# Decays of a state-space mixer: one prefix sum as rows, fetched by transfers, for TensorE products per group

## The chip, the cores and the metric

The kernel runs on one core of a Trainium2 chip. The metric is the device time of one execution in microseconds (us). Before the change three runs gave 3154.31, 3154.56 and 3155.26 us, with a median of 3154.56 us.

## The reference, cut to what matters

The program is one inference step of a hybrid decoder layer on 256 prompt tokens (two chunks of 128) and 8 samples of 8 tokens (64 rows), together 320 token columns. The part around the change is the chunked scan of the Mamba-2 mixer, with 64 heads in 8 groups of 8:

```python
Acum = jnp.cumsum(dt * A.reshape(G, R), axis=2)
seg = Acum[:, :, :, None] - Acum[:, :, None]
Lmat = jnp.exp(jnp.where(causal, seg, -jnp.inf))
CB = jnp.einsum('bclgn,bcsgn->bclsg', Cm, Bm)
Wm = CB[..., None] * Lmat * dt[:, :, None]
y_diag = jnp.einsum('bclsgr,bcsgrp->bclgrp', Wm, x)
decay_end = jnp.exp(Acum[:, :, -1:] - Acum)
...
y_off = jnp.einsum('bclgn,bcgrpn,bclgr->bclgrp', Cm, h_prev, jnp.exp(Acum))
```

Two tables of decays are needed for every group. The first is `exp(Acum[l] - Acum[s])` for all pairs of tokens of a chunk: for each head a matrix with s on the partitions and l along the row. Its raw material is the row `Acum[l]`, repeated on every partition, less a per-partition value `Acum[s]`. The second is `exp(Acum[l])`, one row per head, repeated on the 64 partitions of the head. Projections around the scan are plain matrix products; the rest of the layer (short convolution, mixing, ConvFFN, gated embedding, norms) is not touched.

## The kernel before, in words

Every large product runs as three matmuls (lines 1351 to 1353): weights and activations are each split into a high part (`whi`, `n_hi`, `c_hi`) and a low part (`wlo`, `n_lo`, `c_lo`). Weights arrive in pieces of 128x1024 values (512 KB) in a ring of four slots. SyncE issues the loads (line 540), ScalarE makes the high part three pieces ahead of their use (line 595), VectorE the low part (line 874).

The program is a list of segments, each a list of steps, and each engine walks the same list in order; semaphores join them. The order is written out by hand in `ssm_steps`. One pass of the segment "ssm" handles one group: six units x0 to x5 (a unit is one tile of 128 output columns of the input projection, two weight pieces, 48 matmuls), in the middle of them the norm and the eight output products of the group before, then

unit z0, step `ssd1`, unit z1, steps `ssd2` and `ssd3`, `pair` 0, unit z2, `pair` 1, unit z3, `pair` 2, `pair` 3.

Group 0 is written out; groups 1 to 7 are a loop. Per engine, the steps around the change do this:

- TensorE in `ssd1` transposes x (line 1604) and B (1608), forms C times B (1612), and runs `quad` 0. A `quad` (line 1499) is the row `Acum[l]` of four heads on all partitions, made by multiplying a broadcast column of `hcol` with the triangular mask `tri`. In `ssd2` it runs `quad` 1 to 4 and the sums for `ea` (lines 1633 and 1634). In `ssd3` it forms the chunk states (1641 to 1645). In `pair` it transposes two old states (1655), then waits for `w_ready` and forms y_diag (1667), the new sample states (1676) and y_off (1683, 1688).
- VectorE in `ssd1` scales x into `xdt`, `xwf` and `xwe` (line 923, seven operations), masks C times B (`cbm`, 1033 and 1035), subtracts the column for quad 0 (`quad_min`, line 947) and spreads B (`bblk`, 1038). In `ssd2` it does `quad_min` for quads 1 to 4 and multiplies the exponentials with `cbm` into the weights `wm` (1050). Its part of a unit x is a four-tap convolution (914, 917, 919).
- ScalarE in `ssd2` takes the exponential of `wm` (757) and of `ea` (762).
- GpSimd in `pair` multiplies old states with the last columns of `ea` (1283).

## Time and profile before

| quantity | value |
|---|---|
| median of three runs | 3154.56 us |
| span of the profiled execution | 3152.0 us |
| TensorE matmul busy | 3051.6 us (97%) |
| VectorE busy | 1747.5 us (55%) |
| ScalarE busy | 1155.4 us (37%) |
| GpSimd busy | 235.8 us (7%) |
| mean granted TensorE clock | 0.987 |
| bytes moved | 445.44 MB, mean 141 GB/s |
| HBM written | 25.33 MB |

The span is from the first to the last instruction of the one profiled execution. The page gives no other time for that execution; the median of the unprofiled runs lies 2.56 us above its span. A fp32 matmul shows as two records of TensorE. Records of neighbours overlap, since matmuls are pipelined, so what one costs is read from the distance between starts, not from its length. The chain that ended last lies 93% on TensorE.

### The profile page before, as it was taken

To read this page: it belongs to the slowest core of one execution; us is meant where nothing else is said; L and a number is where in the kernel's file an instruction comes from. 1 tells how busy PE (TensorE), PEld (TensorE's weight loads), DVE (VectorE), ACT (ScalarE), POOL (GpSimd) and SP (SyncE) were. 2 spreads that over 40 slices of the span, in tenths; PEclk is the share of its full clock that TensorE was granted. 3 is DMA by queue.
4 is the path that set the end of the run, shared out by engine and by line. 5 is a ranking of instruction groups with operands and counts; after the bars stand their busy time and mean duration, and the time that the engine had idled before them with its cause. 6 is when DMAs were issued, how large, how long until landed. Compare 5 with 4: busy or idle time off the path is not lost.

```text
span 3152.0 us, 54097 instructions
## 1 busy us (share of the span) xinstructions
PE 3051.6 (97%) x20531; PEld 2948.7 (94%) x20531; DVE 1747.5 (55%) x2346; ACT 1155.4 (37%) x1643; POOL 235.8 (7%) x418
## 2 busy tenths in 40 slices
PE   4999999999999999999999999999999999999988
PEld 2989999898989899999999999999999999999988
DVE  3756556565657565455555555565555555555564
ACT  2443433333434333333333333443333333333443
POOL 1020111101010101000000000100000000000110
PEclk9999999999999999999999999999999999999989
DMA  4544545453544445555555555445555455555443
GB/s 120 134 125 124 159 113 161 111 153 109 158 122 136 124 124 181 150 149 155 147 146 147 147 156 142 143 130 153 152 148 146 146 151 150 152 146 147 146 137 113
DMA packets 749596, 445.44 MB, mean 141 GB/s; under 512 B 18154, under 2 KB 746450, under 8 KB 748754
## 3 DMA queue, kind: packets, MB, share of 16 engines
q1 hardware_dynamic: 668488, 396.17, 44.3%
q10 hardware_dynamic: 80969, 47.21, 5.2%
q8 instruction: 113, 1.85, 0.2%
q14 instruction: 26, 0.21, 0.0%
HBM read 417.99 MB, written 25.33 MB: 141 GB/s over the span
## 4 chain that ended last, share of the span: by engine, by line
PE 93%; DVE 3%; issue 1%; SPq 1%; DMA 1%; ACT 1%; ACTq 0%; POOL 0%; POOLq 0%; DVEq 0%
PE ps L1351 27%; PE ps L1353 27%; PE ps L1352 27%; PE ps L1676 2%; PE ps L1688 2%; PE ps L1667 2%; PE ps L1506 1%; PE ps L1655 1%; PE ps L1633 1%; DMA prow<-in_norm_ple 1%; DVE wlo L874 1%; SPq L528 1%; DVE nt L893 1%; PE ps L1634 1%; PE ps L1683 0%
## 5 line engine op out<-in xcount | busy, mean ns | idle before, releaser
L1351 PE MATMUL ps<-n_hi,whi 128*128 128x320 f32 x4240 | 1325.3, 313 | 35.8 <-DVE n_lo L898 23.1
L1353 PE MATMUL ps<-n_hi,wlo 128*128 128x320 f32 x4240 | 1318.2, 311 | 0.0
L1352 PE MATMUL ps<-n_lo,whi 128*128 128x320 f32 x4240 | 1318.2, 311 | 0.0
L874 DVE TENSOR_TENSOR wlo<-raw,whi 128x1024 fp32r<-128x1024 f32 x747 | 919.6, 1239 | 558.9 <-ACT whi L595 558.6
L595 ACT ACTIVATE whi<-raw 128x1024 fp32r<-128x1024 f32 x747 | 786.3, 1057 | 959.6 <-PE ps L1353 908.6
L1351 PEld LDWEIGHTS ps<-n_hi,whi 128*128 128x128 f32 x4240 | 803.8, 190 | 40.3 <-issue 35.6
L1352 PEld LDWEIGHTS ps<-n_lo,whi 128*128 128x128 f32 x4240 | 804.1, 190 | 0.6
L1353 PEld LDWEIGHTS ps<-n_hi,wlo 128*128 128x128 f32 x4240 | 803.2, 189 | 0.0
L1351 PE MATMUL ps<-c_hi,whi 128*128 128x320 f32 x1728 | 535.6, 310 | 3.1 <-DVE c_lo L910 3.1
L1352 PE MATMUL ps<-c_lo,whi 128*128 128x320 f32 x1728 | 534.6, 309 | 0.0
L1353 PE MATMUL ps<-c_hi,wlo 128*128 128x320 f32 x1728 | 534.6, 309 | 0.0
L1351 PEld LDWEIGHTS ps<-c_hi,whi 128*128 128x128 f32 x1728 | 325.0, 188 | 3.7 <-DVE c_lo L910 3.4
L1352 PEld LDWEIGHTS ps<-c_lo,whi 128*128 128x128 f32 x1728 | 325.1, 188 | 0.0
L1353 PEld LDWEIGHTS ps<-c_hi,wlo 128*128 128x128 f32 x1728 | 325.0, 188 | 0.0
L1092 DVE TENSOR_TENSOR xt<-xt,ps 128x640 f32<-128x640 f32 x120 | 98.4, 820 | 130.5 <-PE ps L1353 130.5
L656 ACT ACTIVATE c_hi<-chunk 128x320 fp32r<-128x320 f32 x76 | 35.9, 472 | 193.1 <-DVE chunk L1151 84.5
L1283 POOL TENSOR_TENSOR hn<-h,ea 128x512 f32<-128x512 f32 x64 | 76.9, 1226 | 345.9 <-ACT ea L762 186.4
L1092 DVE TENSOR_TENSOR acc_a<-acc_a,ps 128x640 f32<-128x640 f32 x64 | 52.6, 822 | 65.5 <-PE ps L1353 65.5
L783 ACT ACTIVATE zs<-chunk 128x320 f32<-128x320 f32 x32 | 15.1, 470 | 189.5 <-DVE chunk L1068 189.5
L1057 DVE SCALAR_TENSOR_TENSOR chunk<-xs,gd,ps 128x320 f32<-128x320 f32 x32 | 17.5, 547 | 109.7 <-PE ps L1667 109.7
L1237 POOL COPY ftail<-spad 128x18 f32 (+1 forms) x44 | 9.7, 220 | 862.6 <-ACT spad L821 862.6
L914 DVE TENSOR_SCALAR scv<-spad,scol 128x336 f32<-128x336 f32 x44 | 20.2, 460 | 86.3 <-ACT spad L821 86.3
(251 smaller groups left out, 1987.5 us busy)
## 6 DMA issues: line engine op xcount, KB each, us to landing
raw<-in_w_in SPq DMA_DIRECT2D x322, 512.0 KB, 5.2
raw<-in_w_ffn_gate SPq DMA_DIRECT2D x88, 512.0 KB, 4.8
raw<-in_w_ffn_up SPq DMA_DIRECT2D x88, 512.0 KB, 5.0
raw<-in_w_ffn_down SPq DMA_DIRECT2D x88, 512.0 KB, 4.2
raw<-in_w_ssm_out SPq DMA_DIRECT2D x64, 512.0 KB, 4.3
h<-in_state_ssm ACTq DMA_DIRECT2D x32, 512.0 KB, 5.2
out_ssm_sample<-hn ACTq DMA_DIRECT2D x32, 512.0 KB, 5.0
raw<-in_w_sc_out SPq DMA_DIRECT2D x32, 512.0 KB, 3.9
```

Of the source, the lines that this page charges most:

```text
L528: sp.dma_start(prow[lo - block_i * P:hi - block_i * P, block_i, :], flat[(lo - row) * P:(hi - row) * P].rearrange("(r f) -> r f", f=P)).th ...
L595: activate(whi[slot][:], raw[slot][:], copy).then_inc(hi_split, 1)
L656: activate(c_hi[:, j, :], chunk[:, j, :], copy).then_inc(c_hi_ready, 1)
L874: tt(wlo[slot][:], raw[slot][:], whi[slot][:].bitcast(F32), SUB).then_inc(lo_split, 1)
L1092: tt(dst, dst, ps[:, b0:b0 + 2, 0:NT], ADD).then_inc(out_added, 1)
L1283: g_.tensor_tensor(hn[j % 2][:, b, :], h0[j % 2][:, b, :], ea[:, j, P + NS + 4 * half:P + NS + 4 * half + 4].unsqueeze(2) .broadcast_to([P ...
L1351: mm(out, w_h, x_h, start=first, stop=False)
L1352: mm(out, w_h, x_l, start=False, stop=False)
L1353: return mm(out, w_l, x_h, start=False, stop=last)
L1667: last = mm(ps[i * HD:(i + 1) * HD, 6, token_rows(c)], xdt[0:rows, c, h * HD:(h + 1) * HD], wm[0:rows, quad_i, m * rows:(m + 1) * rows], s ...
L1676: mm(ps[:, HN_BANKS[half], :], xwe[0:NS, 2, j * P:(j + 1) * P], bblk[:, 4 * half:4 * half + 4, :].rearrange("p b n -> p (b n)"), start=Tru ...
L1688: last = mm(ps[:, 3, P + b * WINDOW:P + (b + 1) * WINDOW], h0t[:, b, :], bc[:, 1, c0:c0 + WINDOW], start=True, stop=True)
```

## The change

The prefix sums of all 64 heads are formed once, in step `dtab` of group 0, with the head on the partition and the token along the row: three matmuls into PSUM bank 7. ScalarE copies them to `wm[0:64, 2]`, writes their exponential to `wm[0:64, 3]`, and stores both to three new tensors in device memory (`acum`, `acum_s`, `decays`). A new helper `load_decays(g)` fetches, on ScalarE's queue, the rows of a group: 128x2x1024 values and 64x512 values into `wm`, and twice 64x4x200 values into `ea`, each row repeated on all its partitions. For groups 1 to 7 it is called in unit x0 of the group, for group 0 in unit x4. `quad`, `head_sums`, step `ssd2` of TensorE and the exponential of `ea` are gone. `quad_min` now reads and writes `wm` in place, for all five quads, in unit z0, ahead of `ssd1`; the five exponentials move from `ssd2` to `ssd1`. GpSimd's products in `pair` wait for `ea_loaded` in place of `ea_exp`.

```diff
+            def load_decays(g):
+
+                wait(act, yd_done, 4 * g)
+                act.dma_start(wm[:, 0:4, :].rearrange("p (c q) n -> p c (q n)", c=2),
+                              acum.rearrange("(a c) n -> a c n", a=1)[:, :, at(g, 1, HPG * P)]
+                              .broadcast_to([P, 2, HPG * P])).then_inc(acum_loaded, 16)
+                act.dma_start(wm[0:NS, 4, :], acum_s[:, at(g, 1, HPG * NS)].broadcast_to([NS, HPG * NS])
+                              ).then_inc(acum_loaded, 16)
+                wait(act, hd_done, 8 * g)
+                for half in range(2):
+                    of_half = decays.rearrange("o (x a) n -> a o x n", a=2)[half]
+                    act.dma_start(ea[half * HD:half * HD + HD, :, :],
+                                  of_half[:, at(4 * g, 4)].broadcast_to([HD, 4, P + NS + NB])
+                                  ).then_inc(ea_loaded, 16)
...
+                    act.wait_ge(row_sums, 1)
+                    activate(wm[0:HEADS, 2, 0:NT], ps[0:HEADS, 7, 0:NT], copy).then_inc(rows_kept, 1)
+                    activate(wm[0:HEADS, 3, 0:P + NS + NB], ps[0:HEADS, 7, P:NT + NB], ACT.Exp).then_inc(rows_kept, 1)
+                    act.wait_ge(rows_kept, 2)
...
                         load_pair(g, 0)
                         load_pair(g, 1)
+                        if seg.start:
+                            load_decays(g)
+                    if seg.start == 0 and j == 4:
+                        act.wait_ge(rows_saved, 16 * 3)
+                        load_decays(g)
...
-                elif kind == "ssd2":
                     for quad in range(5):
                         act.wait_ge(q_min, 5 * g + quad + 1)
...
-                    wait(act, hd_done, 8 * g)
-                    for half in range(2):
-                        act.wait_ge(ea_done, 2 * g + half + 1)
-                        activate(ea[:, 2 * half:2 * half + 2, :],
...
             def quad_min(g, quad):
-                dve.wait_ge(q_done, 5 * g + quad + 1)
...
-                    last = ts(wm[0:rows, quad, i * width:(i + 1) * width],
-                              ps[0:rows, bank, i * width:(i + 1) * width],
+                    part = wm[0:rows, quad, i * width:(i + 1) * width]
+                    last = ts(part, part,
                               hcol[0:rows, 6 + c, h:h + 1], 0.0, SUB, ALU.min)
...
+                elif kind == "unit" and step[1] == "z":
+                    if j == 0:
+                        dve.wait_ge(hcol_ready, g + 1)
+                        dve.wait_ge(acum_loaded, 32 * (g + 1))
+                        for quad in range(5):
+                            quad_min(g, quad)
...
                 elif kind == "pair":
-                    pool.wait_ge(ea_exp, 2 * g + j // 2 + 1)
+                    pool.wait_ge(ea_loaded, 32 * (g + 1))
...
+                    for c in range(2):
+                        mm(ps[0:HEADS, 7, c * P:(c + 1) * P], dta(c, P), tri[:], start=True, stop=True)
+                    mm(ps[0:HEADS, 7, SEQ:NT + NB], dta(2, NS), tri_s[:], start=True, stop=True).then_inc(row_sums, 1)
...
-                elif kind == "ssd2":
-                    for i, (s, count) in enumerate(((xw_ready, 3 * g + 1), (xw_ready, 3 * g + 2),
-                                                    (xw_ready, 3 * g + 3), (None, 0)), 1):
...
-                        quad(g, i)
...
                     for half in range(2):
-                        if j == 0:
-                            pe.wait_ge(q_min, 5 * g + 5)
-                        else:
+                        if j:
                             pe.wait_ge(t_kept, 8 * g + 2 * (j - 1) + half + 1)
...
                     pe.wait_ge(w_ready, 5 * g + 5)
-                    pe.wait_ge(ea_exp, 2 * g + 2)
+                    pe.wait_ge(cbm_ready, g + 1)
```

Where instructions moved is shown in the listed order of an engine, one row per run of equal instructions. On VectorE the piece from the last of the scaled copies of x to the first operation of `pair` 0 read so before:

```order
L923 TENSOR_TENSOR xwe<-ps,hcol 64x512
L1033 TENSOR_TENSOR cbm<-ps,tri 128x256
L1035 TENSOR_TENSOR cbm<-ps,tri_s 64x64
L947 TENSOR_SCALAR wm<-ps,hcol 128x128 x4
L1038 TENSOR_TENSOR bblk<-bt,tri_s 64x1024
L874 TENSOR_TENSOR wlo<-raw,whi 128x1024 x2
L947 TENSOR_SCALAR wm<-ps,hcol 128x128 x12
L947 TENSOR_SCALAR wm<-ps,hcol 64x64 x8
L1050 TENSOR_TENSOR wm<-wm,cbm 128x512 x4
L1050 TENSOR_TENSOR wm<-wm,cbm 64x512
L1057 SCALAR_TENSOR_TENSOR chunk<-xs,gd,ps 128x320
```

And so it reads now on VectorE, from the subtractions to `bblk` (lines have moved by 27 to 32; behind these rows follow the two low parts of unit z1 and the five products into `wm`, and between them nothing):

```order
L974 TENSOR_SCALAR wm<-wm,hcol 128x128 x16
L974 TENSOR_SCALAR wm<-wm,hcol 64x64 x8
L950 TENSOR_TENSOR xdt<-ps,hcol 128x512
L950 TENSOR_TENSOR xwf<-ps,hcol 128x512
L950 TENSOR_TENSOR xwe<-ps,hcol 128x512
L950 TENSOR_TENSOR xdt<-ps,hcol 128x512
L950 TENSOR_TENSOR xwe<-ps,hcol 128x512
L950 TENSOR_TENSOR xdt<-ps,hcol 64x512
L950 TENSOR_TENSOR xwe<-ps,hcol 64x512
L1066 TENSOR_TENSOR cbm<-ps,tri 128x256
L1068 TENSOR_TENSOR cbm<-ps,tri_s 64x64
L1070 TENSOR_TENSOR bblk<-bt,tri_s 64x1024
```

The 24 subtractions stood behind the scaled copies, 4 in `ssd1` and 20 in `ssd2`. Now all 24 stand in front of them.

On TensorE the end of unit z1 and the start of `ssd2` read so before (the rows of lines 1633 and 1634 then alternate until there are eight of each):

```order
L1351 MATMUL ps<-n_hi,whi 128x320
L1352 MATMUL ps<-n_lo,whi 128x320
L1353 MATMUL ps<-n_hi,wlo 128x320
L1506 MATMUL ps<-tri,hcol 128x128 x12
L1506 MATMUL ps<-tri_s,hcol 64x64 x8
L1633 MATMUL ps<-tri,hcol 64x128
L1634 MATMUL ps<-tri_s,hcol 64x72
```

The same place on TensorE now:

```order
L1381 MATMUL ps<-n_hi,whi 128x320
L1382 MATMUL ps<-n_lo,whi 128x320
L1383 MATMUL ps<-n_hi,wlo 128x320
L1637 MATMUL ps<-xwe,bt 128x512
L1640 MATMUL ps<-bt,xwf 128x128
```

The 36 matmuls of `ssd2` are gone, and `ssd3` follows unit z1 at once.

On ScalarE `ssd1` and unit z1 of group 0 read so before:

```order
L748 ACTIVATE zs<-ps 128x320
L751 ACTIVATE bt<-ps 128x256
L752 ACTIVATE bt<-ps 64x128
L595 ACTIVATE whi<-raw 128x1024 x2
L748 ACTIVATE zs<-ps 128x320
L757 ACT_TABLE_LOAD
L757 ACTIVATE wm<-wm 128x512 x4
L757 ACTIVATE wm<-wm 64x512
L762 ACTIVATE ea<-ps 128x400 x2
L767 ACTIVATE h1t<-ps 128x512
```

And so now:

```order
L783 ACTIVATE zs<-ps 128x320
L786 ACTIVATE bt<-ps 128x256
L787 ACTIVATE bt<-ps 64x128
L791 ACT_TABLE_LOAD
L791 ACTIVATE wm<-wm 128x512 x4
L791 ACTIVATE wm<-wm 64x512
L600 ACTIVATE whi<-raw 128x1024 x2
L783 ACT_TABLE_LOAD
L783 ACTIVATE zs<-ps 128x320
L794 ACTIVATE h1t<-ps 128x512
```

The five exponentials have moved ahead of the high parts of unit z1, and the two exponentials of `ea` are gone.

## Rows read from the trace of the kernel before

**Rows 1.** The page, part 1: busy time, share of the span, instructions

```profile
PE 3051.6 (97%) x20531; PEld 2948.7 (94%) x20531; DVE 1747.5 (55%) x2346; ACT 1155.4 (37%) x1643; POOL 235.8 (7%) x418
```

**Rows 2.** Waits of TensorE: who waited <- for whom: us in total, times, longest

```profile
PE ps L1351 <- issue: 10.9, 6, 2.0
...
PE ps L1351 <- DVE wlo L874: 1.1, 1, 1.1
```

**Rows 3.** Timeline of TensorE, group 3: start us, length us, instructions

```profile
572.03 1.47 PE L1604 MATMUL ps<-ident,xs 128*128 128x128 f32 x12
...
574.46 1.16 PE L1506 MATMUL ps<-tri,hcol 128*128 128x128 f32 x8
575.38 0.39 PE L1351 MATMUL ps<-n_hi,whi 128*128 128x320 f32 x1
...
582.49 2.84 PE L1506 MATMUL ps<-tri,hcol 128*128 128x128 f32 x24
...
591.34 1.12 PE L1641 MATMUL ps<-xwe,bt 128*128 128x512 f32 x2
...
595.06 1.74 PE L1667 MATMUL ps<-wm,xdt 128*64 128x128 f32 x12
```

**Rows 4.** Timeline of VectorE, group 3

```profile
566.22 1.19 DVE L917 SCALAR_TENSOR_TENSOR cv<-xpad,gcol,cv 128x344 f32<-128x344 f32 x2
567.45 0.58 DVE L919 SCALAR_TENSOR_TENSOR cv<-xpad,gcol,cv 128x344 f32<-128x344 f32 x1
...
569.80 1.22 DVE L874 TENSOR_TENSOR wlo<-raw,whi 128x1024 fp32r<-128x1024 f32 x1 [0.64 <-ACT whi L595]
572.66 0.69 DVE L923 TENSOR_TENSOR xdt<-ps,hcol 128x512 f32<-128x512 f32 x1 [1.64 <-PE ps L1604]
...
577.32 1.11 DVE L947 TENSOR_SCALAR wm<-ps,hcol 128x128 f32<-128x128 f32 x4
578.36 1.21 DVE L1038 TENSOR_TENSOR bblk<-bt,tri_s 64x1024 f32<-64x1024 f32 x1
579.49 2.34 DVE L874 TENSOR_TENSOR wlo<-raw,whi 128x1024 fp32r<-128x1024 f32 x2
583.58 4.72 DVE L947 TENSOR_SCALAR wm<-ps,hcol 128x128 f32<-128x128 f32 x20 [1.75 <-PE ps L1506]
588.22 3.08 DVE L1050 TENSOR_TENSOR wm<-wm,cbm 128x512 f32<-128x512 f32 x5
```

**Rows 5.** Groups of VectorE by shape: busy us, mean ns | idle before

```profile
L990 DVE SCALAR_TENSOR_TENSOR wm<-wm 64x320 f32<-64x320 f32 x6 | 2.9, 483 | 0.2
...
L988 DVE TENSOR_SCALAR wm<-wm 64x320 f32<-64x320 f32 x1 | 0.3, 319 | 0.0
```

**Rows 6.** Group of ScalarE by shape

```profile
L757 ACT ACTIVATE wm<-wm 128x512 f32<-128x512 f32 x32 | 19.3, 626 | 4.8 <-DVE wm L947 4.7
```

**Rows 7.** GpSimd in group 3, and its products by line (min/median/max ns)

```profile
566.20 0.18 POOL L1275 COPY gnrm<-ptab 128x4 f32 x1
589.69 5.52 POOL L1283 TENSOR_TENSOR hn<-h,ea 128x512 f32<-128x512 f32 x4 [23.30 <-ACT ea L762]
...
L1283 POOL TENSOR_TENSOR hn<-h,ea x64: 1034/1040/2676, 160.3 to 1203.4; 128x512 f32<-128x512 f32 x64
```

**Rows 8.** GpSimd and VectorE at 2030 us, where both add at once

```profile
2030.78 1.58 POOL L1297 TENSOR_TENSOR sq_sum<-sq_sum,sig_b 128x640 f32<-128x640 f32 x1 [2.66 <-ACT sig_b L633]
...
2031.68 1.76 DVE L874 TENSOR_TENSOR wlo<-raw,whi 128x1024 fp32r<-128x1024 f32 x1 [1.02 <-ACT whi L595]
```

**Rows 9.** Stretches of 12 us behind two loop boundaries; the column behind POOL is TensorE's clock

```profile
348.20:360.20 12.00, 11.94 (x71) 11.95 (x72) 3.39 (x4) 3.71 (x6) 1.80 (x7) 0.86 0.59 160
...
1070.50:1082.50 12.00, 11.99 (x63) 12.00 (x64) 2.45 (x2) 3.15 (x6) 1.42 (x5) 0.75 0.52 138
```

**Rows 10.** Timeline of TensorE: behind a short idle time, and at a boundary

```profile
2062.58 0.38 PE L1351 MATMUL ps<-n_hi,whi 128*128 128x320 f32 x1 [1.24 <-DVE n_lo L898]
2062.80 0.30 PE L1352 MATMUL ps<-n_lo,whi 128*128 128x320 f32 x1
...
492.42 0.41 PE L1351 MATMUL ps<-n_hi,whi 128*128 128x320 f32 x1 [1.73 <-issue]
```

**Rows 11.** Issues of transfers: count, KB each, median us to landing

```profile
gain_rows<-in_norm_final ACTq DMA_DIRECT2D x1, 1024.0 KB, 5.4
...
dcol<-in_ssm_d ACTq DMA_DIRECT2D x2, 8.0 KB, 34.5
```

More of the change, by code:

```diff
@@ L145, in hybrid_decoder @@
 def hybrid_decoder(nc, ins, outs, scratch):
+    acum = nc.dram_tensor("acum", (2, HEADS * P), F32, kind="Internal").ap()
+    acum_s = nc.dram_tensor("acum_s", (1, HEADS * NS), F32, kind="Internal").ap()
+    decays = nc.dram_tensor("decays", (1, HEADS, P + NS + NB), F32, kind="Internal").ap()
     ctx = ExitStack()
@@ L191, in s1 @@
             return ssm.enter_context(nc.sbuf_tensor(name, shape, dt))
-        N_KC = 13
+        N_KC = 10
         heads_tab = s1("heads_tab", [P, GROUPS, N_KC, HPG])
@@ L280, in hybrid_decoder @@
         SUMS = (None, 4, 5, 6, 7)
-        QUADS = ((0, 7), (0, 2), (1, 3), (1, 4), (2, 5))
+        CHUNK_OF = (0, 0, 1, 1, 2)
         HN_BANKS = (7, 2)
@@ L940, in quad_min @@
             def quad_min(g, quad):
-                dve.wait_ge(q_done, 5 * g + quad + 1)
-                c, bank = QUADS[quad]
+                c = CHUNK_OF[quad]
                 rows, width, n = (P, P, 4) if quad < 4 else (NS, NS, 8)
@@ L1002, in keep @@
                                       ps[:, bank, 0:2 * HEADS].rearrange("p (c g h) -> p c g h", c=2, g=GROUPS))
-                        return v.tensor_copy(heads_tab[0:NS, :, kc + 2, :],
-                                             ps[0:NS, bank, 2 * HEADS:3 * HEADS].rearrange("p (g h) -> p g h", g=GROUPS))
+                        v.tensor_copy(heads_tab[0:NS, :, kc + 2, :],
+                                      ps[0:NS, bank, 2 * HEADS:3 * HEADS].rearrange("p (g h) -> p g h", g=GROUPS))
                     keep(0, 2)
-                    keep(9, 3).then_inc(a_kept, 1)
+                    v.tensor_copy(wm[:, 4, 0:2 * HEADS], ps[:, 3, 0:2 * HEADS])
+                    v.tensor_copy(wm[0:NS, 4, 2 * HEADS:3 * HEADS], ps[0:NS, 3, 2 * HEADS:3 * HEADS]
+                                  ).then_inc(a_kept, 1)
                     dve.wait_ge(dt_sums, 1)
@@ L1029, in tasks @@
                         if c == 0:
-                            xchunk(xwf[:], c, hcol[:, 12, :], rows)
+                            xchunk(xwf[:], c, hcol[:, 9, :], rows)
                         xchunk(xwe[0:rows, c, :], c, hcol[0:rows, 3 + c, :], rows).then_inc(xw_ready, 1)
@@ L1040, in tasks @@
                 elif kind == "ssd2":
-                    for quad in range(1, 5):
-                        quad_min(g, quad)
                     dve.wait_ge(cbm_ready, g + 1)
@@ L1045, in tasks @@
                         dve.wait_ge(q_exp, 5 * g + quad + 1)
-                        c = QUADS[quad][0]
+                        c = CHUNK_OF[quad]
                         rows, n = (P, 4) if quad < 4 else (NS, 8)
@@ L1493, in turn_tails @@
                 last.then_inc(tail_turned, 1)
-            def head_sums(c, h, rows, width):
-                return hcol[0:rows, 9 + c, h:h + 1].broadcast_to([rows, width])
-            def quad(g, i):
-                c, bank = QUADS[i]
-                rows, n = (P, 4) if i < 4 else (NS, 8)
-                mask = tri[:] if i < 4 else tri_s[:, 0:NS]
-                for m in range(n):
-                    h = (4 * (i % 2) if i < 4 else 0) + m
-                    last = mm(ps[0:rows, bank, m * rows:(m + 1) * rows], head_sums(c, h, rows, rows), mask,
-                              start=True, stop=True)
-                last.then_inc(q_done, 1)
             def tasks(seg, it, step, pos):
@@ L1586, in dta @@
                     def dta(c, rows):
-                        return heads_tab[0:rows, :, 9 + c, :]
+                        return wm[0:rows, 4, c * HEADS:(c + 1) * HEADS]
                     for bank, inner, inner_s in ((4, tri[:], tri_s[:, 0:NS]), (5, after[:], after_s[:])):
@@ L1599, in tasks @@
                         pe.wait_ge(heads_ready, 1)
+                        pe.wait_ge(rows_kept, 2)
                     wait(pe, out_added, 8 * g)
@@ L1614, in tasks @@
                     last.then_inc(cb_done, 1)
-                    pe.wait_ge(hcol_ready, g + 1)
-                    quad(g, 0)
-                elif kind == "ssd2":
-                    for i, (s, count) in enumerate(((xw_ready, 3 * g + 1), (xw_ready, 3 * g + 2),
-                                                    (xw_ready, 3 * g + 3), (None, 0)), 1):
-                        if s is not None:
-                            pe.wait_ge(s, count)
-                        if i == 3:
-                            pe.wait_ge(bt_kept, g + 1)
-                        quad(g, i)
-                    pe.wait_ge(cbm_ready, g + 1)
-                    pe.wait_ge(q_min, 5 * g + 1)
-                    for half in range(2):
-                        for i in range(2):
-                            q = 2 * half + i
-                            c0 = i * (P + NS + NB)
-                            for h in range(2):
-                                dst = ps[h * HD:(h + 1) * HD, 6 + half, :]
-                                mm(dst[:, c0:c0 + P], head_sums(1, 2 * q + h, P, HD), tri[:], start=True, stop=True)
-                                last = mm(dst[:, c0 + P:c0 + P + NS + NB], head_sums(2, 2 * q + h, NS, HD), tri_s[:],
-                                          start=True, stop=True)
-                        last.then_inc(ea_done, 1)
                 elif kind == "ssd3":
```

22 lines of the change are left out of this document (12 added, 10 removed).

## The prediction

> **What bounds the kernel now.** I read the busy times first: TensorE is busy for 3051.6 us of a span of 3152.0, VectorE for 55% and ScalarE for 37% [rows 1]. Then the waits of TensorE: inside the eight groups it waits for no other engine. Its only idle times there are six pauses at the loop's boundaries, 10.9 us together, which stand as "issue"; for a split weight it waited once in the whole kernel, for 1.1 us [rows 2]. So in the groups every matmul taken out shortens the span by its own distance to the next start, as long as nothing else becomes late. Last I laid TensorE's timeline of group 3 beside VectorE's [rows 3, 4]; the other groups run alike. The reader is to see there that VectorE finished the weights `wm` at 588.22 + 3.08 = 591.30 while TensorE wanted them at 595.06: a spare time of 3.76 us, and 9.77 us of TensorE's work is taken out in front of that point.
>
> **Removed from TensorE.** `quad` 0 lies between 574.46 and 575.38 (0.92 us), `ssd2` between 582.49 and 591.34 (8.85 us) [rows 3]. Together 9.77 us per group, 78.2 us for eight groups, all on the path that sets the end.
>
> **Added to TensorE.** Three matmuls once. Twelve records of the transposes take 1.47 us at most [rows 3], so a matmul of two records some 0.25 us, and three about 0.7 us. It sits in `dtab`, before TensorE's next unit, so it counts in full. The wait for `rows_kept` comes after six more steps and is long over.
>
> **VectorE's chain to w_ready.** This is where the gain is partly lost. First when TensorE wants the weights now: `ssd1` ends at 574.46, unit z1 takes 582.49 - 575.38 = 7.11 us, `ssd3` and the transposes of `pair` 0 take 595.06 - 591.34 = 3.72 us, so it asks at 585.29 [rows 3]. Now VectorE. Its first free moment in unit z0 is the end of the low part at 569.80 + 1.22 = 571.02; before it idled there for 1.64 us until the transposes came [rows 4]. From there the work is one row without a wait, since all it reads is there:
> - 24 subtractions. From PSUM, twenty of them (12 wide, 8 narrow) took 4.64 us from 583.58 to 588.22, and four wide ones 1.04 us [rows 4]: 0.26 us a wide one, about 0.19 us a narrow one, 5.7 us in all. From SBUF they may stream twice as fast. The trace shows the kind of operation: 320 elements by a one-source operation in SBUF took 319 ns, by a two-source one 483 ns [rows 5]. 483 - 319 = 164 ns saved on 320 elements is 0.5 ns an element, hence 66 ns on 128 and 33 ns on 64. That makes 16 x 0.19 + 8 x 0.16 = 4.3 us. I take 4.3 and keep 5.7 as the upper end.
> - seven scaled copies and `cbm`: 577.32 - 572.66 = 4.66 us.
> - `bblk`: 579.49 - 578.36 = 1.13 us; two low parts: 2.34 us; five products into `wm`: 3.08 us [rows 4].
>
> The sum is 4.3 + 4.66 + 1.13 + 2.34 + 3.08 = 15.51 us, which ends at 586.53: TensorE waits 1.24 us. At 5.7 us it waits 2.6 us. The copies for `ssd3` end at 571.02 + 4.3 + 4.2 = 579.5, before TensorE asks for them at 581.57.
>
> The Trainium skill, page "VectorE: DVE Perf Modes", section "Mode 2×_2P — use both read ports for one tensor", says that a one-source fp32 operation from SBUF to SBUF gives two results per cycle, and that one from PSUM cannot. The 319 against 483 ns of this trace agree [rows 5]. By the page the subtractions are the 4.3 us case, without it the 5.7 us case.
>
> **GpSimd comes earlier.** Its four products of `pair` 0 and 1 waited 23.30 us for `ea` and ran from 589.69 on [rows 7]. With `ea` fetched long before, the first starts when the copy at 566.20 is done, at about 566.4, in the middle of VectorE's convolution of x5 [rows 4, 7]. The trace shows that the two hold each other up. GpSimd's product takes 1034 ns alone but up to 2676 ns [rows 7]; and a low part that met an addition of GpSimd at 2031.68 took 1.76 us instead of 1.22 us, the extra time being what was left of the addition that ran until about 2032.3 [rows 4, 8]. Between the convolution's operations VectorE waits for its own result, and there GpSimd can step in: two such places are left, between the operations that start at 566.22 and the one at 567.45, so two products of 1.04 us delay the end of the convolution from 568.03 to 570.1. The two low parts then end at about 572.4 instead of 571.02, since 0.64 us of the delay is idle time anyway [rows 4]. Back-to-back VectorE operations leave no such place; the other two products run beside the scaled copies. I take 1.4 us; the bounds are 0 (GpSimd always gives way) and about 3.1 us (all four in front, 4.16 us less 0.64 and the 0.4 that two low parts overlap with). The wait per group becomes 1.24 + 1.4 = 2.6 us, 21 us in eight groups.
>
> The Trainium skill, page "SBUF — State Buffer", section "Who interferes with whom", speaks against this change: GpSimd and a VectorE operation with two SBUF inputs, or in the two-port mode, exclude each other, and who starts first keeps the port for the whole operation. The rows above agree [rows 7, 8]. By it the subtractions and GpSimd's products cannot run together either.
>
> **TensorE's clock.** At the loop's boundaries TensorE pauses for 1.7 to 2.0 us, and behind each of the six the granted clock falls to 1.2 GHz, half of its 2.4: in the 12 us behind it the mean is about 0.86 in four of them and about 0.75 in two, as in the two rows shown [rows 9]. Time lost is 12 x 0.14 = 1.7 us or 12 x 0.25 = 3.0 us, 2.1 us in the mean. A pause of 1.24 us in dense work left the clock as it was: the next start comes 0.22 us later, not double [rows 10]; the smallest pause at a boundary was 1.73 us [rows 10]. A wait of 2.6 us in each group lies above both, so I expect the fall there too: 8 x 2.1 = 16.8 us.
>
> **What lies beside other work.** ScalarE issues four more transfers per group in unit x0, and waits for nothing new there (`yd_done` and `hd_done` of the group before are long counted). Queued behind them are the filling of x0 and two high parts, both needed only two units later: nothing. In group 0 it waits at x4 for the stores issued in `dtab`, two units earlier. The five exponentials now stand before two high parts: 5 x 0.63 = 3.1 us [rows 6] from the end of `bt`, over before VectorE asks at about 582. The removed exponentials of `ea` were not on the path. The transfers: 1024 + 128 + 400 = 1552 KB per group. The nearest row, one row of 8 KB repeated on 128 partitions, moved 1024 KB in 5.4 us [rows 11], so about 8.2 us. `acum` has all the units and output products from x0 to z0 for that, in group 0 unit x5 and half of z0, about 10.6 us by the 7.11 us of a unit. The weight loads share the engines, but a piece is split three pieces (3 x 3.55 us) ahead of its use. I take 0 with 0 and some 2 us in group 0 as bounds.
>
> **The sum.** -78.2 + 0.7 + 21 + 16.8 = -39.7 us against the profiled execution's span of 3152.0, which lies 2.6 us under the median of the runs. On the median: 3154.6 - 39.7 = 3115 us.
>
> **The rivals.**
> - *Wait without a fall of the clock.* The pause lies behind dense work of unit z1 and not behind two pairs in a row, as the boundaries do. For it: 1.24 us did no harm [rows 10]. Against: six of six at 1.7 us and more [rows 9]. -78.2 + 0.7 + 21 = -56.5: 3098 us.
> - *GpSimd gives way*, and the subtractions are fast: wait 1.24 us, no fall. For it: VectorE's five products at 588.22 were not held up though GpSimd arrived among them. Against: row 2031.68. -78.2 + 0.7 + 9.9 = -67.6: 3087 us.
> - *No wait at all.* VectorE is faster than added up. -77.5: 3077 us.
> - *The subtractions are not faster from SBUF.* Wait 1.24 + 1.4 + 1.4 = 4.0 us, clock falls: 8 x 6.1 = 49 us: 3126 us.
> - *Slower: the repeated rows hold the weights up.* Two small transfers with repeated rows, 8 KB each, took 34.5 us to land [rows 11], in pieces of four bytes. If `load_decays` holds the shared engines so long, TensorE runs out of pieces split ahead after 3 x 3.55 = 10.7 us and waits 23.8 us per group, against a net gain of 5.0 us: 8 x 18.8 = +150 us, 3305 us. It decides from 10.7 + 5.0 = 15.7 us on; I reckon with 8.2. Runs of 800 bytes and 4 KB speak against it.
>
> **How the numbers follow.** Forecast with wait and fall of clock 0.40; wait alone 0.20; GpSimd gives way 0.22; no wait 0.06; slow subtractions 0.08; slower by starved weights 0.03; a gain lost altogether 0.01. The point is the likeliest, 3115 us. The range reaches from the third case, 3085, to just under the slow subtractions, 3124, and leaves out about 0.18. All upper ends at once (subtractions slow, all four products in front) would be a wait of 5.7 us with the fall, 3139 us; I give that under 0.02, within the slow subtractions. A measurement of this kernel tells 0.2% (6 us) from no change; faster by more 0.96, within 0.01, slower 0.03.
>
> **What would show it.** Right: TensorE idles before the first matmul of y_diag in `pair` 0, released by VectorE's product into `wm`, eight times, 2 to 3 us each; the clock column is near half behind it; VectorE's wide subtractions start about 0.19 us apart instead of 0.26; GpSimd's products start during x5, and a convolution operation there lasts 1 us longer. Wrong: no such wait, or one before `ssd3`; a wait of TensorE on a low part with ScalarE waiting for `raw`; VectorE waiting for `wm` from the transfer in z0; the clock untouched behind the wait.

## The result: 22.8 us slower

| | us |
|---|---|
| before, median of 4 runs beside it | 3154.45 |
| after, median of 4 runs (3175.93 to 3179.03) | 3177.21 |
| ratio, 95% interval | 1.0075 (1.0061 to 1.0089) |
| span of the profiled execution, before and after | 3152.0 and 3177.3 |
| mean granted TensorE clock, before and after | 0.987 and 0.972 |

The forecast was 3115 us, in a range of 3085 to 3124. The change costs 0.75% where it was to bring 1.3%.

The first view is the busy times of the kernel after. TensorE has 634 instructions fewer than before [rows 1], but its busy time fell by 27.3 us, not by the 78 that the removed products took.

```profile
PE 3024.3 (95%) x19897; PEld 2921.7 (92%) x19897; DVE 1759.6 (55%) x2346; ACT 1144.5 (36%) x1629; POOL 241.8 (8%) x418
```

The second is TensorE's waits after (who waited <- for whom: us in total, times, longest).

```profile
PE ps L1546 <- DMA prow<-in_norm_ple: 29.5, 1, 29.5
PE ps L1381 <- DVE n_lo L925: 25.1, 6, 11.4
PE ps L1661 <- DVE wm L1080: 24.2, 8, 3.1
PE ps L1381 <- DVE wlo L901: 20.0, 8, 3.7
PE ps L1381 <- issue: 10.7, 6, 2.0
...
PE ps L1637 <- DVE xwe L950: 2.6, 8, 0.5
```

Three of them stand inside the groups and are new. The wait for `wm` ahead of y_diag was forecast (21 us, measured 24.2). The wait for a low part, `wlo`, was 1.1 us in all before [rows 2] and is 20.0 now. The wait for `xwe` ahead of `ssd3` is small.

The third is the clock. These are stretches of group 3 after: length, busy time (and count) of PE, PEld, DVE, ACT and POOL, then TensorE's granted clock, DMA share and GB/s.

```profile
591.00:602.00 11.00, 10.70 (x74) 9.85 (x73) 11.00 (x32) 8.53 (x14) 0.00 (x0) 1.00 0.26 68
602.00:606.00 4.00, 0.98 (x10) 0.74 (x9) 3.65 (x6) 1.62 (x3) 0.00 (x0) 1.00 0.76 207
606.00:620.00 14.00, 14.00 (x50) 10.72 (x49) 3.55 (x8) 1.53 (x2) 0.00 (x0) 0.51 0.16 44
620.00:627.00 7.00, 7.00 (x51) 6.54 (x50) 2.19 (x2) 2.58 (x4) 2.04 (x2) 1.00 0.99 283
```

Before the wait the clock is full, 2.4 GHz. Behind it TensorE runs 14 us at half, 1.2 GHz, and "busy" hides that: the engine is busy for 14.00 of 14.00 us and does half the work. The kernel before, in the same place:

```profile
595.00:609.00 14.00, 14.00 (x94) 12.05 (x93) 5.65 (x9) 5.86 (x9) 0.20 (x1) 1.00 0.41 113
```

I read the clock of every 1-us window from 0 to 1400 us, which holds all eight groups, and added up what was missing to 1.00, as a span "lost" at half clock. The kernel before lost 22.2 us there, the kernel after 76.8. Between them are 54.6 us, and 52.9 us is what the eight stretches behind the wait for `wm` lost: 6.8 us each in seven groups, 5.1 in group 6. Two things bound this measure. Lost time counts only where TensorE works; in these eight stretches it works throughout. And the rest of the span has losses of its own, 18.8 us before and 12.3 after.

The timeline of TensorE in that place shows what ran in them. The six matmuls of y_diag (twelve records) stand behind the wait. The two matmuls of the new states (four records) took 1.98 us before and 3.78 now, the last eight of y_off 1.88 and 3.48.

```profile
598.91 1.12 PE L1637 MATMUL ps<-xwe,bt 128*128 128x512 f32 x2 [0.30 <-DVE xwe L950]
...
601.65 1.04 PE L1649 MATMUL ps<-ident,h 128*128 128x128 f32 x8
605.71 2.42 PE L1661 MATMUL ps<-wm,xdt 128*64 128x128 f32 x12 [3.02 <-DVE wm L1080]
608.05 3.78 PE L1670 MATMUL ps<-bblk,xwe 64*128 64x512 f32 x4
...
612.35 3.48 PE L1682 MATMUL ps<-bc,h0t 128*128 128x43 f32 x16
```

From the first product of y_diag (605.71) to the first product of z2 (615.62) pair 0 now takes 9.91 us; at full clock, in the kernel with both moves below, it takes 5.61. Full clock is back only at 620.06, 4.4 us after z2 began.

VectorE and GpSimd did most of what the prediction laid out. This is VectorE, and under it GpSimd. The 24 subtractions take 4.44 us, the wide ones 0.196 us apart and the narrow ones 0.163. GpSimd's products, now at 583.19, fall into the convolution, whose operations take 1.85 and 1.24 us for 1.19 and 0.58 [rows 4], and also into the two low parts, which stand back to back: 4.04 us for 2.34.

```profile
583.07 1.85 DVE L944 SCALAR_TENSOR_TENSOR cv<-xpad,gcol,cv 128x344 f32<-128x344 f32 x2
584.96 1.24 DVE L946 SCALAR_TENSOR_TENSOR cv<-xpad,gcol,cv 128x344 f32<-128x344 f32 x1
586.12 4.04 DVE L901 TENSOR_TENSOR wlo<-raw,whi 128x1024 fp32r<-128x1024 f32 x2
590.08 4.51 DVE L974 TENSOR_SCALAR wm<-wm,hcol 128x128 f32<-128x128 f32 x24
594.52 0.67 DVE L950 TENSOR_TENSOR xdt<-ps,hcol 128x512 f32<-128x512 f32 x1
...
602.57 3.08 DVE L1080 TENSOR_TENSOR wm<-wm,cbm 128x512 f32<-128x512 f32 x5
```

```profile
583.19 5.88 POOL L1313 TENSOR_TENSOR hn<-h,ea 128x512 f32<-128x512 f32 x4
```

The wait for `wlo` begins on ScalarE, in unit x0 of the next group. First ScalarE before, then after:

```profile
647.27 1.04 ACTq L600 DMA_DIRECT2D h<-in_state_ssm  x2
648.36 0.39 ACT L737 ACTIVATE xpad<-ps 128x256 f32<-128x256 f32 x1 [3.83 <-issue]
```

```profile
662.75 1.04 ACTq L605 DMA_DIRECT2D h<-in_state_ssm  x2
664.04 1.17 ACTq L611 DMA_DIRECT2D wm<-acum  x1
665.46 0.51 ACTq L614 DMA_DIRECT2D wm<-acum_s  x1
666.14 1.40 ACTq L619 DMA_DIRECT2D ea<-decays  x2
667.59 0.38 ACT L772 ACTIVATE xpad<-ps 128x256 f32<-128x256 f32 x1 [7.58 <-issue]
```

The four issues put the copy into `xpad` off by 7.58 - 3.83 = 3.75 us. Behind it VectorE has the convolutions, the norm and only then the low parts of x2:

```profile
675.63 2.15 DVE L1103 RECIPROCAL var<-var 128x320 f32<-128x320 f32 x1
...
680.18 1.69 DVE L1110 TENSOR_TENSOR c_lo<-chunk,c_hi 128x320 fp32r<-128x320 f32 x4
681.79 2.35 DVE L901 TENSOR_TENSOR wlo<-raw,whi 128x1024 fp32r<-128x1024 f32 x2
```

```profile
683.06 0.41 PE L1381 MATMUL ps<-n_hi,whi 128*128 128x320 f32 x1 [2.50 <-DVE wlo L901]
```

So of the 3.75 us 2.50 became a wait, and 1.25, the difference, were spare.

The sum against the span before: removed work -77.5 (net of the 0.7 us added), `wm` +24.2, `wlo` +18.9, `xwe` +2.6, and +6.8 for two waits outside the groups: for `prow` at the start (29.5 against 24.7 us) and for `n_lo` (25.1 against 23.1, nearly all of it behind 2000 us). For the clock the whole span counts: 89.1 us lost after and 41.0 before. Of these 10.5 and 11.7 us fall on time in which TensorE is idle, where they cost nothing. That leaves 78.6 and 29.3, so +49.3. The sum is +24.3; the spans differ by +25.3. Why the kernel after lost less behind 1400 us is not shown; over the fourteen profiles that part varies from 12 to 21 us.

### The profile page after: what moved, and what is told of

Same layout as the page of the kernel before. It is cut to its first block, busy times and chain, and to the rows that moved or that the text cites. A ratio compares the mean times of both kernels' runs of the same rounds, so it can differ in the third digit from the quotient of the medians.

```text
span 3177.3 us, 52855 instructions
## 1 busy us (share of the span) xinstructions
PE 3024.3 (95%) x19897; PEld 2921.7 (92%) x19897; DVE 1759.6 (55%) x2346; ACT 1144.5 (36%) x1629; POOL 241.8 (8%) x418
## 3 DMA queue, kind: packets, MB, share of 16 engines
q8 instruction: 106, 1.74, 0.2%
## 4 chain that ended last, share of the span: by engine, by line
PE 82%; DVE 10%; issue 3%; ACTq 1%; SPq 1%; ACT 1%; DMA 1%; POOL 0%; DVEq 0%; POOLq 0%
PE ps L1381 25%; PE ps L1382 24%; PE ps L1383 24%; DVE wlo L901 2%; PE ps L1670 2%; PE ps L1682 2%; PE ps L1661 2%; DVE wm L974 1%; DVE cv L944 1%; SPq L533 1%; DVE wm L1080 1%; DVE nt L920 1%; PE ps L1649 1%; DMA prow<-in_norm_ple 1%; PE ps L1677 0%
## 5 line engine op out<-in xcount | busy, mean ns | idle before, releaser
L1381 PE MATMUL ps<-n_hi,whi 128*128 128x320 f32 x4240 | 1333.4, 314 | 56.5 <-DVE n_lo L925 25.1
L901 DVE TENSOR_TENSOR wlo<-raw,whi 128x1024 fp32r<-128x1024 f32 x747 | 933.0, 1256 | 566.0 <-ACT whi L600 565.7
L1661 PE MATMUL ps<-wm,xdt 128*64 128x128 f32 (+1 forms) x384 | 60.0, 285 | 24.2 <-DVE wm L1080 24.2
L1661 PEld LDWEIGHTS ps<-wm,xdt 128*64 128x64 f32 (+1 forms) x384 | 40.8, 142 | 44.7 <-DVE wm L1080 26.1
L1670 PE MATMUL ps<-bblk,xwe 64*128 64x512 f32 x128 | 77.7, 736 | 0.0
```

The lines of the kernel that those rows point to most:

```text
L901: tt(wlo[slot][:], raw[slot][:], whi[slot][:].bitcast(F32), SUB).then_inc(lo_split, 1)
L1381: mm(out, w_h, x_h, start=first, stop=False)
L1661: last = mm(ps[i * HD:(i + 1) * HD, 6, token_rows(c)], xdt[0:rows, c, h * HD:(h + 1) * HD], wm[0:rows, quad_i, m * rows:(m + 1) * rows], s ...
L1670: mm(ps[:, HN_BANKS[half], :], xwe[0:NS, 2, j * P:(j + 1) * P], bblk[:, 4 * half:4 * half + 4, :].rearrange("p b n -> p (b n)"), start=Tru ...
```

## The experiments

The theory: the loss is the wait for `wm`, the half clock behind it, which costs twice as much as the wait (52.9 and 24.2 us), and the wait that comes from the issues in x0. Rivals: the clock falls because the dense products are gone, wait or no wait; or the transfers' traffic costs.

**The issues moved.** ScalarE's issues leave x0 for the output steps.

```
-                        if seg.start:
-                            load_decays(g)
...
+                elif kind == "out" and seg.name == "ssm":
+                    if j == 0:
+                        load_rows(g)
+                    if j == 2:
+                        load_ends(g)
```

> Only the place of the four transfer issues of groups 1 to 7 changes: from unit x0 to the output steps (the two of wm in step out 0, the two of ea in step out 2), where ScalarE waits 2.46 us per step for TensorE. Theory (the loss of the change is made of a 3.0 us wait of TensorE for wm in pair 0, a stretch at half clock behind it that costs 6.8 us a group, and a 2.5 us wait for wlo in unit x2 that comes from the issues in x0): the wlo wait (20.0 us, 8 times) goes in seven groups, the wm wait and its stretch stay: 3177 - 7 x 2.5 = 3160 us, 3158 if the one extra fall near 978 us goes too. Rival (the traffic of the repeated rows is what costs, wherever it is issued): 3172 to 3182.

Measured 3153.75 us, ratio 1.0000 (0.9991 to 1.0009): 23 us better than the kernel after, so as long as the kernel before. That is 4 to 6 us more than expected. The wait for `wlo` is down to 1.1 us, once, which is 18.9 us; another 2.8 us are shorter waits for `prow` and `n_lo`, and 3 us less are lost to the clock. The wait for `wm` stands as it was.

```profile
PE ps L1672 <- DVE wm L1091: 24.2, 8, 3.1
...
PE ps L1392 <- DVE wlo L912: 1.1, 1, 1.1
```

**The subtractions moved.** VectorE does one quad in each of the steps out 3 to out 7, where it waited 1.2 us and more for TensorE; ScalarE's exponentials follow one step behind.

```
-                    if j == 0:
+                    if j == 0 and not seg.start:
                         dve.wait_ge(hcol_ready, g + 1)
...
+                    if seg.name == "ssm" and 3 <= j:
+                        dve.wait_ge(hcol_ready, g + 1)
+                        dve.wait_ge(acum_loaded, 32 * (g + 1))
+                        quad_min(g, j - 3)
```

> Only the place of the 24 subtractions and five exponentials of groups 1 to 7 changes: subtractions from unit z0 to steps out 3 to out 7, one quad each, exponentials from ssd1 to out 4 to out 7 and x5; issues stay in x0. Theory: in seven groups the waits for wm and xwe (3.0 and 0.3 us) go, and with them the stretch at half clock (6.8 us of the span each): 3177 - 7 x 10.1 = 3106 us, and the granted clock of the groups is back near 0.98. Rival (the clock falls because the dense products of the decays are gone and transposes and short products alone stand in pair 0, wait or no wait): only the waits go, 3177 - 7 x 3.3 = 3154 us, and the half-clock stretch stays. Rival on traffic: no better than 3150.

Measured 3109.27 us, 0.9861 (0.9846 to 0.9876), near the 3106 us of the theory. The wait for `wm` stands only in group 0, and so does the stretch; the clock lost to 1400 us is 29.0 us in place of 76.8. TensorE has none of the dense products here, and the clock stays up: that rival falls.

```profile
PE ps L1395 <- DVE wlo L911: 19.2, 8, 3.5
...
PE ps L1675 <- DVE wm L1090: 3.1, 1, 3.1
```

**Both moved.** The edits of the two kernels above, together; ScalarE's part of them in the output steps:

```
+                    if j == 0:
+                        load_rows(g)
+                    if j == 2:
+                        load_ends(g)
+                    if j >= 4:
+                        exps(g, j - 4)
```

> Both moves of the two kernels before: issues in the output steps, subtractions and exponentials there too. Theory: the two gains add, 3177 - 71 - 18 = 3088 us, 66 below the kernel before. Rival of the missing dense products: 3177 - 23 - 18 = 3136 us. Rival on traffic: not below 3150.

Measured 3091.11 us, 0.9802 (0.9788 to 0.9815). The gains of 23.5 and 67.9 us add but for 5 us. Pair 0 at full clock, 571 to 578 us:

```profile
571.00:578.00 7.00, 7.00 (x46) 5.11 (x45) 2.52 (x6) 1.51 (x3) 0.00 (x0) 1.00 0.26 68
```

**The wait filled.** The kernel after, nothing moved; idle time is turned into work that nobody reads.

```
+                    if j == 0:
+                        pe.wait_ge(z_ready, 4 * g + 1)
+                        for k in range(20):
+                            mm(ps[:, 0, 0:NT], n_hi[:, k % 16, 0:P], n_hi[:, k % 16, :], start=True, stop=True)
                     pe.wait_ge(w_ready, 5 * g + 5)
```

> The changed kernel with 20 products of 128x128 by 128x320 (2.7 us at full clock), whose result nobody reads, put ahead of TensorE's wait for the weights in pair 0, every group; nothing is moved. Theory (the idle wait is what lowers the clock): the time spent there stays the same, since the filler fits in the wait of 3.0 us, but the half-clock stretch of 6.8 us goes in all eight groups: 3177 - 55 = 3122 us. Rival (the sparse work behind lowers the clock): 3177 us, the stretch stays. A middle result would say that both count.

Measured 3131.82 us, 0.9926 (0.9912 to 0.9939): 45 us gained by adding work, where 55 were expected. All eight stretches are gone (25.6 us lost to 1400 us), and from the transposes to y_diag still pass 3.02 us. The missing 10 us are the clock elsewhere: it fell behind four of the waits for `wlo` in place of two, and behind 1400 us it lost 18.2 us in place of 12.3. Over the whole span the loss while TensorE works goes from 78.6 to 32.9 us, a gain of 45.7. It is faster than the kernel before though VectorE is as late as in the kernel after. In group 3:

```profile
600.00:614.00 14.00, 14.00 (x95) 12.10 (x93) 5.65 (x9) 4.30 (x8) 2.92 (x3) 1.00 0.59 160
```

**How long a wait, in the same place.** Three kernels take the one with both moves and make `wm` late again with repeated operations on VectorE, in groups 1 to 7. The first has two, as here; the second has `range(3)`; the third has one whole and one of half the width (`for n in (NB, NB // 2)`, on `bblk[:, 0:n]`).

```
+                    if seg.start:
+                        dve.wait_ge(bblk_ready, g + 1)
+                        for _ in range(2):
+                            own(tt(bblk[:], bt[0:NS, 2, :].unsqueeze(1).broadcast_to([NS, NB, P]),
+                                   tri_s[:, NS:NS + NB].unsqueeze(2).broadcast_to([NS, NB, P]), MUL))
```

> The kernel with both moves (3091 us), with two spread operations on VectorE (1.2 us each) repeated ahead of the products that make wm, in groups 1 to 7: wm, which lay ready 0.85 us before TensorE asked, comes late, and TensorE waits some 1.5 us in pair 0, with transposes and short products behind it. It asks how long the wait must be for the half-clock stretch. If the cost is in proportion to the wait: stretch of 3.4 us, 3091 + 7 x (1.5 + 3.4) = 3125 us. If a wait of that length does nothing to the clock, as the pause of 1.24 us in the trace before did nothing: 3091 + 10 = 3101 us. If any visible wait brings the whole stretch: 3091 + 7 x 8.3 = 3149 us.

> The same with three repeated operations: a wait of some 2.6 us in pair 0 of groups 1 to 7, nothing moved, no issue in x0. Theory (a wait of this length in pair 0 brings 14 us at half clock, whatever else the change does): 3091 + 7 x (2.6 + 6.8) = 3157 us. Rival (the fall needed the crowd of the change, such as GpSimd and the late chain): only the waits, 3091 + 18 = 3109 us.

> As the kernel with two repeated operations ahead of wm, but the second one half as wide (0.65 us in place of 1.2): a wait of some 1.1 us in pair 0 of groups 1 to 7 in place of 1.74. It asks where between 0 and 1.74 us the stretch begins. If a wait of this length does nothing to the clock: 3091 + 8 = 3099 us. If the stretch comes whole: 3091 + 7 x (1.1 + 6.1) = 3141 us. In proportion to 1.74 us: 3091 + 7 x (1.1 + 3.9) = 3126 us.

| wait in pair 0, groups 1 to 7 | groups with a long stretch | lost there | median us | ratio |
|---|---|---|---|---|
| none (both moved) | 0 of 7 | 0 | 3091.11 | 0.9802 |
| 1.2 us | 1 of 7 | 5.1 us | 3103.62 | 0.9842 (0.9826 to 0.9859) |
| 1.74 us | 7 of 7 | 5.1 or 6.8 us (42.7 in all) | 3137.09 | 0.9932 (0.9908 to 0.9956) |
| 2.99 us | 7 of 7 | 6.8 us (47.8 in all) | 3151.03 | 0.9987 (0.9977 to 0.9996) |

Waits and groups are those of the one profiled execution, times are medians. The cost of the clock is a step and not a slope: it comes between 1.2 and 1.74 us, and from 1.74 to 2.99 us it grows by 5 us in all seven groups. The step is not sharp. With 1.2 us one group fell and six did not, at the same wait; and with 1.74 us the profiled run is the slowest of four (3141.62 us at a mean clock of 0.972), while another took 3124.82 us at 0.977, in which probably not all seven groups fell. None of the three times forecast for 1.74 us (3101, 3125, 3149) was met. The end of the wait and the stretch behind it, with 1.74 us (first fence), and stretches with 1.2 us (second fence, one group with the fall and one without):

```profile
588.00:590.00 2.00, 1.60 (x12) 1.19 (x12) 0.35 (x1) 0.30 (x1) 0.00 (x0) 1.00 0.31 82
590.00:601.00 11.00, 11.00 (x39) 8.38 (x39) 3.29 (x7) 0.95 (x2) 0.00 (x0) 0.53 0.01 2
```

```profile
304.00:315.00 11.00, 11.00 (x40) 8.95 (x39) 3.45 (x8) 1.53 (x2) 0.00 (x0) 0.53 0.06 10
...
444.00:456.00 12.00, 12.00 (x80) 10.69 (x80) 5.66 (x9) 2.99 (x5) 0.00 (x0) 1.00 0.34 97
```

In these kernels the issues do not stand in x0 nor, in groups 1 to 7, the subtractions in z0: the stretch needs neither, a wait of this length in this place is enough.

In all 26 stretches in pair 0 of these three kernels and the kernel after, full clock came back only in the dense unit z2, 2.5 to 5.6 us after its first product. So the short matmuls all ran at half clock from the fall on.

**The same wait ahead of dense work.** TensorE is held ahead of unit z2 in place of pair 0, until VectorE's last operation of pair 0, put off by four repeated operations (not shown), is through.

```
+                    if seg.start and step[1] == "z" and step[-1] == 2:
+                        pe.wait_ge(yg_ready, 4 * g + 1)
                     unit(seg, it, step, pos)
```

> The kernel with both moves, with TensorE held ahead of unit z2 of groups 1 to 7 until pair 0's last VectorE operation is through, which is put off by four repeated operations: a wait of some 2.8 us, like the one of the changed kernel, but with 48 dense products (7 us) behind it in place of short ones. Theory (the stretch is long because sparse work stands behind the wait): the stretch is short, as behind the loop's boundaries, 1.7 to 3.4 us a group: 3091 + 7 x (2.8 + 2.5) = 3128 us. Rival (the length of the wait alone sets it): 3091 + 7 x (2.8 + 6.8) = 3158 us.

Measured 3124.1 us, 0.9904 (0.9887 to 0.992). The wait is 2.93 us, as long as the one of 2.99, but each group loses 3.4 us and not 6.8, and 27 us lie between the two kernels. Group 3 of the kernel with 2.99 us, with the first product of z2 in the second row:

```profile
592.66 2.97 PE L1690 MATMUL ps<-wm,xdt 128*64 128x128 f32 x12 [2.99 <-DVE wm L1105]
...
603.12 0.61 PE L1410 MATMUL ps<-n_hi,whi 128*128 128x320 f32 x1
```

And the wait and group 3 here:

```profile
PE ps L1406 <- DVE chunk L1119: 20.5, 7, 2.9
```

```profile
590.90 0.63 PE L1406 MATMUL ps<-n_hi,whi 128*128 128x320 f32 x1 [2.94 <-DVE chunk L1119]
```

```profile
589.00:597.00 8.00, 6.09 (x26) 6.10 (x27) 2.86 (x6) 1.53 (x2) 0.06 (x1) 0.57 0.55 153
597.00:604.00 7.00, 7.00 (x47) 5.87 (x47) 2.48 (x2) 2.58 (x4) 1.98 (x2) 1.00 0.44 127
```

Here the clock falls already in the wait, at 589.2 us, and the short matmuls of pair 0 now stand ahead of it; that they are the reason is not shown. Of the 6.8 us at half clock 1.3 to 1.9 are idle and cost nothing. What a group really loses is 2.6 us on average, against 6.7 in the other kernel, which makes 28 us in seven groups and accounts for the 27. The two kernels differ in what stands ahead of the wait as well as behind it, so they do not part these two. That sparse work behind it draws the loss out is what the rows above add: 9.9 us for pair 0 in place of 5.6.

**Group 0 mended too.** Its rows are issued in x3, its subtractions stand in x4.

```
-                    if seg.start == 0 and j == 4:
+                    if seg.start == 0 and j == 3:
                         act.wait_ge(rows_saved, 16 * 3)
-                        load_decays(g)
+                        load_rows(g)
+                    if seg.start == 0 and j == 4:
+                        load_ends(g)
...
+                    if seg.start == 0 and j == 4:
+                        dve.wait_ge(hcol_ready, g + 1)
+                        dve.wait_ge(acum_loaded, 32 * (g + 1))
+                        for quad in range(5):
+                            quad_min(g, quad)
```

> The kernel with both moves, and group 0 mended too: its rows of wm are issued in unit x3 in place of x4, its 24 subtractions stand in x4 in place of z0. The last wait for wm (3.1 us) and the last stretch at half clock (6.8 us) go: 3091 - 10 = 3081 us. Rival: the loads are not there in time for x4, VectorE holds up conv and low parts, and the wait only changes its place: 3088 to 3095 us.

Measured 3079.99 us, 0.9759 (0.9743 to 0.9776). This is the fastest of all: 73.5 us below the kernel before. Its span, 3079.4, lies 72.6 below that before. Over the whole span both lose 29.3 us to the clock while TensorE works, and TensorE waits 4.1 us longer here (92.5 against 88.4 us in all), so the removed work of 77.5 us should show as 73.4.

**More traffic.** Two more transfers of repeated rows a group, written to device memory and not to the tiles, so reading and writing it. In bytes they are more than the change itself added, 14.7 MB against 12.7.

```
+                    if j in (1, 3):
+                        wait(act, spare_loaded, 16 * (2 * (g - 1) + j // 2))
+                        act.dma_start(spare.rearrange("p (c n) -> p c n", c=2),
...
+                                      .broadcast_to([P, 2, HPG * P])).then_inc(spare_loaded, 16)
```

> The kernel with both moves and group 0 mended (3080 us), with two more transfers of 1024 KB a group for groups 1 to 7, from the same repeated rows into an unused tensor of device memory, issued by ScalarE in steps out 1 and out 3 where it waits for TensorE: 14.7 MB more, against 12.7 MB that the change added. Theory (the transfers cost nothing in themselves): 3076 to 3084 us. Rival (they take room from the weights, whose 512 KB are wanted every 3.5 us): the two transfers of a group take some 5 us of the 16 engines together, and TensorE would wait for weights up to that: 3090 to 3115 us.

Measured 3091.61 us, 0.9793 (0.9773 to 0.9813), 11.6 above the same kernel without them. The four runs spread from 3081.43 to 3098.77 us, the profiled one is the slowest, and the interval overlaps a little with that of the kernel without them (0.9743 to 0.9776). So the size is uncertain, but the kind of loss is plain in the profile. Here the theory was wrong: traffic is free only up to a point. ScalarE waited 6.6 to 9.3 us for a piece of weights once in each of seven groups, here 7.23, and TensorE waited behind it, 12.4 us in seven groups:

```profile
523.88 1.06 ACT L603 ACTIVATE whi<-raw 128x1024 fp32r<-128x1024 f32 x1 [7.23 <-DMA raw<-in_w_ssm_out]
```

```profile
PE ps L1411 <- DVE acc_a L1148: 12.4, 7, 3.1
```

Without the extra transfers ScalarE waits for these weights too, but less (45.3 us in all in place of 87.7, and 26.1 in the kernel before), and TensorE has no such wait. So what the change itself moves is still hidden, with less to spare.

**The issues behind the copy.** As with the subtractions moved alone, but in x0 the issues stand behind the copies into `xpad`.

```
-                        if seg.start:
-                            load_decays(g)
                     unit_ps = ps[:, j % 2, :]
...
+                    if j == 0 and seg.start:
+                        load_decays(g)
```

> The kernel with the subtractions moved alone (3109 us), whose four issues stay in unit x0 of groups 1 to 7 but stand behind the copies into xpad instead of ahead of them. Theory (the wlo wait of 2.5 us in x2 comes from the issues' 4 us ahead of the copy into xpad, which put off convolution, norm and low parts on VectorE): the wait goes, 3109 - 18 = 3091 us. Rival (it comes from the transfers' traffic in x0, which puts off the weights of the next pieces, or from the time that they take on ScalarE's queue wherever in x0 they stand): 3105 to 3112 us.

Measured 3091.35 us, 0.9804 (0.9788 to 0.982), 18 us better. The transfers start in the same unit; only the copy no longer stands behind them. So it was the place in ScalarE's order, and neither traffic nor the unit. The wait for `wlo` is 4.9 us in all in place of 19.2 (it is 1.1 in the kernel with both moves; where the other 3.8 us come from stays open):

```profile
PE ps L1395 <- DVE wlo L911: 4.9, 8, 1.1
```

**One step of the order.** The kernel after, with unit z2 ahead of pair 0.

```
-                          ("pair", 0), ("unit", "z", 2), ("pair", 1), ("unit", "z", 3)
+                          ("unit", "z", 2), ("pair", 0), ("pair", 1), ("unit", "z", 3)
```

> The changed kernel with one step moved in all groups: unit z2 stands ahead of pair 0 in place of behind it; issues and subtractions stay as the change put them. Theory: the weights wm have 7 us more, the wait of 3.0 us and the half-clock stretch go in all eight groups: 3177 - 24 - 55 = 3098 us if pair 1, now straight behind pair 0, waits for nothing new. Rival (the wait comes back in pair 1, for ScalarE's copies of the old states and VectorE's sums, and lowers the clock there): 3120 to 3177 us.

Measured 3104.23 us, 0.9845 (0.9829 to 0.9862): 73 us below the kernel after by one line, where 79 were expected. The wait for `wm` is gone in all groups, with it the stretch, and none came for pair 1; the `wlo` wait stayed, as it should:

```profile
PE ps L1381 <- DVE wlo L901: 19.2, 8, 3.6
```

## Why the prediction was wrong

The miss is 3177.3 - (3152.0 - 39.7) = 65.0 us, span against span. By its own steps:

- **TensorE's clock:** this is the step that failed. "8 x 2.1 = 16.8 us" took the price of the fall from the loop's boundaries, and the place has its own: the eight stretches lost 52.9 us. That the clock falls was right; for how long was carried over from a place where a dense unit stands behind the pause. Behind this wait stand pair 0's short matmuls, and full clock came back only in z2. The kernels with a wait of the same length before pair 0 and before z2 lose 6.8 and 3.4 us a group, of which 6.7 and 2.6 us while TensorE works. With 3.6 us less lost elsewhere than before, the step is off by 32.5 us.
- **ScalarE's issues:** "both needed only two units later: nothing" also failed, by 18.9 us. The low parts are needed two units later, but behind the copy in VectorE's order stand two convolutions and the norm's chain as well, and the spare time there was 1.25 us. I looked at the transfers' users and did not follow the queue behind the issuing instruction.
- **VectorE's chain and GpSimd:** right in kind and nearly in size, 3.0 us a group for 2.6, off by 3.2 us in the sum. The subtractions took 4.44 us for 4.3. GpSimd delayed the low parts more than forecast: they ended 1.2 us behind the start of `ssd1` (590.08 and 588.88), before 1.0 us ahead of it, a shift of 2.2 us where I took 1.4. That "back-to-back VectorE operations leave no such place" was wrong: the two low parts took 4.04 us for 2.34 beside GpSimd. The rule on GpSimd and VectorE (the Trainium skill, "SBUF — State Buffer", "Who interferes with whom") agrees with the rows after. The copies for `ssd3`, said to be in time, were reckoned without this shift; they were 0.3 us late, 2.6 us in all.
- **Removed and added work:** right. With the new waits and stretches out of the way 72.6 us of the 77.5 arrive, and the longer waits outside the groups take 4.1 of the rest.
- **Traffic:** right for this change. The 1024 KB for `wm` took 7.7 us to land (median of 8), where I reckoned with 8.2 for all 1552 KB of a group. The kernel with somewhat more than twice the extra bytes lost time.
- **The rest:** 6.8 us lie in waits for `prow` and `n_lo` outside the groups. They vary between the profiles (the same wait for `prow` is 23.9 to 29.5 us in the fourteen profiles); that they have nothing to do with the change is likely but not shown. With 1.0 us left over the steps make up the 65.0.

Of the rivals the slow subtractions came nearest, with 3126 us, but their reason did not hold: the subtractions were fast. None priced the fall higher than the boundaries did, and that is why the range was too narrow: its upper end moved with the wait, and the clock term in it was a constant. "Slower" stood at 0.03, and only for starved weights, which did not come.

## What to carry to other kernels

A wait of TensorE can cost more than itself: ask what stands around it. Here 3.0 us of waiting ahead of short matmuls cost 6.8 us more, because the clock fell and came back only in the next dense unit. So put VectorE's late work where TensorE runs dense units, or let a dense unit stand between it and its use: that one line gained 73 us. Where nothing can move, useless matmuls in the gap were still better than idling here, by 45 us. And an issue of a transfer is an instruction on its engine: follow what stands behind it there, down to TensorE. Last, a busy time does not tell of the clock: TensorE was busy for 14.00 of 14.00 us at half clock.

## What the runs showed of the chip that I had not expected

- In one and the same place, waits of 1.2 us brought the half clock in one group of seven, waits of 1.74 us in seven of seven (one profiled execution each); from there to 2.99 us the time lost to the clock grew by only 5 us in seven groups.
- In the kernel after, seven waits of 2.5 to 3.7 us between dense units (`wlo` in x2) lowered the clock twice only, with 1.7 us lost each time; seven waits of 1.74 us ahead of short matmuls lost 5.1 us or 6.8 each.
- Full clock never came back during pair 0's short matmuls, in 26 stretches that began there; without a wait ahead of them the same matmuls did not lower it (5.61 us at full clock in the seven groups of the kernel with both moves).
- An issue of a transfer with repeated rows held ScalarE for 0.5 to 1.2 us (1.17 for the rows of `wm`, 0.51 for the short ones, 1.40 for the two of `ea` together), and four of them put off the next operation by 3.75 us.
